# Semaphores cleared by ranges of numbers, and attention's gate steps laid by a written table

## The chip, the cores and the metric

One core of a Trainium2 chip runs the whole program. The metric is the device time of one execution in microseconds (us), as the median of several runs. The engines are named as the profile names them: PE multiplies matrices, PEld is its weight load, DVE is the vector engine, ACT the scalar engine, POOL the GpSimd engine, and SP only issues DMAs and handles semaphores.

## The reference, cut to what matters

The program is one layer of a sequence model: 2048 tokens of width 1024 are normalised, projected, mixed by three branches (pooling, differential attention, a state-space layer), gated, projected out, and sent through 32 experts. The change touches the attention stage and what stands between the stages.

```python
def block(args):                       # 16 blocks of 128 queries, 4 heads, 2 maps each
    qi, i = args
    s = jnp.einsum('bqhmd,bkhmd->bhmqk', qi, kf)
    p = jax.nn.softmax(jnp.where(mask, s, -1e30), axis=-1)
    a = p[:, :, 0] - lam * p[:, :, 1]
    return jnp.einsum('bhqk,bkhe->bqhe', a, vf)
o = lax.map(block, (qb, jnp.arange(nb)))
o = rmsnorm(o, subln_g) * (1.0 - lambda_init)
...
ga, gb, gc = jnp.split(jax.nn.sigmoid(h @ gate_w[l] + gate_b[l]), N_BRANCHES, axis=-1)
mixed = ga * (ya @ proj_a[l]) + gb * (yb @ proj_b[l]) + gc * (yc @ proj_c[l])
```

The mask is causal by blocks, so block i of queries meets keys 0 to 128 (i + 1) only. The product `h @ gate_w` doesn't depend on attention, and half of it is computed inside the attention stage.

## The kernel before, in words

**Stages.** Six stages follow one another: project, attention, pooling, ssm, out, moe. Each has its own semaphores and ends with `Stage.end` (L134): the engines have met at the end of the stage's block, SP clears each semaphore of the stage by an instruction of its own (L136), and all engines meet again (L137). Nothing of the next stage is issued before that. Semaphore numbers are handed out as they are asked for. The six stages hold 72, 36, 20, 47, 52 and 39 semaphores, whose numbers form 1, 1, 1, 2, 2 and 2 runs without a gap (project has 99 to 170; ssm has 153 to 170 and 227 to 255; moe has 171 to 204 and 222 to 226).

**Attention.** For each of 4 heads there are 16 items i (128 queries each). An item's keys are cut into pieces of up to 512, so item i has i // 4 + 1 pieces, and a head 40. In the step of item i, PE does this: the gate steps of the step's first slot; a wait until DVE has weighed item i (`weighed`, from L544); then, for each piece, the transposes of the item's scores (L321, into banks 4 and 5), perhaps up to two pieces of scores of item i + 2 (L311, banks 0 to 3), the gate steps of this piece's slot, and the product of the piece before with the values (L332, bank 6), which waits until ACT has copied the transposed piece (`place`, L437).

**The other engines in a step.** ACT goes in a fixed order: `take` of the last item (L442, L445); then, for each piece, `place`; behind it every `gate_out` that has come due (L420: it waits for the sum of 8 gate steps, and after every second one `w_high` rounds the next weights, L414); behind the first piece the exponentials of item i + 1 for map 1, and behind the second piece (or the only one) those for map 0 (L429). DVE reads scores out of the banks (L520, L523), takes maxima (L531, L532), turns the sums of the exponentials into factors (L539, L540) and weighs item i + 1 (L544); `lower` (L557) makes the low part of new gate weights.

**Gate steps.** One gate step is three matmuls of 512 columns (L344 to L346); 8 steps make a unit, which is summed in bank 7, and a head has 12 units. The first step of a unit waits until ACT has emptied bank 7 (`gate_placed`). `gate_plan` (L166) lays out how many steps stand in which slot: 8 ahead of item 0, 72 within the items, 8 behind item 15 and 8 behind the transposes of the outputs. A unit ends in these slots before (item, slot): (1,0) (2,0) (3,0) (4,2) (6,1) (7,2) (10,2) (13,1) (15,4). Slot 0 stands ahead of the wait for `weighed`, slot j ahead of the product of piece j - 1.

**Between heads.** PE does the 8 gate steps, then the scores of the next head's items 0 and 1, waits until DVE has read them out, waits for the normed outputs (`o_normed`, from L601), transposes them into banks 0 to 3 (L402), does 8 gate steps, and transposes the next head's values in four groups over banks 4 and 5 (`turn_v`, L358). Group 2 waits until ACT has copied group 0 out (L450). ACT does `take`, the square root (L488), `gate_out`, the exponentials, then the copies of the transposed outputs (L498).

**SP.** It stores gates and loads the next gate weights into one buffer (`load_w`, L256, in `store_gates`). At unit `units_by(NT - 3)` of a head it first waits until all scores of the head are made and then issues 16 loads of 256 KB for the next head's queries and keys (L252; in the last head two loads of 2 MB, L278 and L279). That unit is 9 before.

Of the kernel before, what the change touches and what calls it, by code (L numbers as in the profile page):

```python
# [25 lines left out]
KD = D // P  # L26
NT = T // P
TB = T // 512
EPS = 1e-6
HEADS = 4  # L30
# [74 lines left out]
class Stage:  # L105
# [26 lines left out]
        return s.__enter__()  # L132

    def end(self):  # L134
        for s in self.sems:
            self.nc.sync.sem_clear(s)  # L136
        self.nc.all_engine_barrier()  # L137


# [26 lines left out]
def gate_plan():  # L166


    wanted = [7] * 4 + [5] * 4 + [3] * 8
    first, last = KD, 2 * KD  # L170
    slots, placed, owed = [], first, 0
    total = 12 * KD
    for i in range(NT):
        n = i // 4 + 2
        row = []
        for j in range(n):
            owed += wanted[i] / n
            room = KD - placed % KD
            take = min(int(owed + 1e-6), room, total - last - placed)
            if i == NT - 1 and j == n - 1:  # L180
                take = min(total - last - placed, room)
            row.append(take)
            placed += take
            owed -= take
        slots.append(row)
    return first, slots


def stage_attention(nc, g, h_hi, h_lo, late_hi, late_lo, wt):

    RING = 3
    CH, NU = 6, 12
# [22 lines left out]
    with Stage(nc, "att") as s:  # L215
# [27 lines left out]
        with nc.Block() as block:  # L243
# [53 lines left out]
            @block.tensor  # L297
            def _(pe):
                def score(h, p):
                    i, c, width, _ = pairs[p]  # L300
                    gp = NP * h + p
                    if c == 0 and i % 4 == 0:
                        pe.wait_ge(qk_ready[i // 4], 64 * (h + 1))
                    if gp >= 2:
                        pe.wait_ge(q["evacuated"], 2 * gp - 2)
                    if h >= 1 and p in (2, 3):
                        pe.wait_ge(q["o_split"], 4 * h)
                    for a, b in ((q_hi, k_hi), (q_hi, k_lo), (q_lo, k_hi)):
                        for m in range(2):
                            own = slice(m * DH, (m + 1) * DH)  # L310
                            mm = pe.matmul(bank[p % 2 * 2 + m][:, :width], a[own, i * P:(i + 1) * P],  # L311
                                           b[own, c * 512:c * 512 + width], start=b is k_hi and a is q_hi, stop=a is q_lo)
                            if a is q_lo:
                                mm.then_inc(q["scored"], 1)

                def turn_a(h, n):
                    i, c, blocks = turn_units[n]
                    if n >= 2:
                        pe.wait_ge(q["a_placed"], NP * h + n - 1)
                    for j in range(blocks):  # L320
                        mm = pe.transpose(bank[4 + n % 2][:, j * P:(j + 1) * P],  # L321
                                          S[:, (NT * h + i) % RING, 0, (4 * c + j) * P:(4 * c + j + 1) * P], const(g, "ident"))
                    mm.then_inc(q["a_turned"], 1)

                def weigh_v(h, n):
                    i, c, blocks = turn_units[n]
                    if c == 0 and NT * h + i >= 1:
                        pe.wait_ge(q["o_copied"], NT * h + i)
                        pe.wait_ge(q["o_squared"], NT * h + i)
                    pe.wait_ge(q["a_placed"], NP * h + n + 1)  # L330
                    for j in range(blocks):
                        mm = pe.matmul(bank[6][:, 0:P], aT[:, n % 2, j, :], val[:, 4 * c + j, :],  # L332
                                       start=4 * c + j == 0, stop=4 * c + j == i)
                    mm.then_inc(q["summed"], 1)

                def gate(gn):
                    gu, k = gn // KD, gn % KD
                    c, tb = gu // 2, gu % 2
                    b, at = c % 2, slice(tb * 512, (tb + 1) * 512)
                    if k == 0 and tb == 0 and c >= 1:  # L340
                        pe.wait_ge(q["w_split"], c)
                    if k == 0 and gu >= 1:
                        pe.wait_ge(q["gate_placed"], gu)
                    pe.matmul(bank[7][:], w_hi[b][:, k, :], h_hi[:, k, at], start=k == 0, stop=False)  # L344
                    pe.matmul(bank[7][:], w_hi[b][:, k, :], h_lo[:, k, at], start=False, stop=False)  # L345
                    mm = pe.matmul(bank[7][:], w_lo[b][:, k, :], h_hi[:, k, at], start=False, stop=k == KD - 1)  # L346
                    if k == KD - 1:
                        mm.then_inc(q["gate_summed"], 1)

                def turn_v(h):  # L350
                    pe.wait_ge(q["v_ready"], 16 * (h + 1))
                    for t in range(TB):
                        if t >= 2:
                            pe.wait_ge(q["v_placed"], TB * h + t - 1)
                        elif h >= 1:
                            pe.wait_ge(q["a_placed"], NP * h - 1 + t)
                        for j in range(4):
                            mm = pe.transpose(bank[4 + t % 2][:, j * P:(j + 1) * P],  # L358
                                              vT[:, t * 512 + j * P:t * 512 + (j + 1) * P], const(g, "ident"))
                        mm.then_inc(q["v_turned"], 1)  # L360

                done = 0
                for h in range(HEADS):
                    if h >= 1:
                        turn_v(h)
                    while done < NU * KD * h + first_fill:
                        gate(done)
                        done += 1
                    if h == 0:
                        for p in range(first_pair[2]):  # L370
                            score(0, p)
                        turn_v(0)
                    pe.wait_ge(q["v_placed"], TB * (h + 1))
                    for i in range(NT):
                        ahead = list(range(first_pair[i + 2], first_pair[i + 3])) if i + 2 < NT else []
                        lo, hi = first_pair[i], first_pair[i + 1]
                        for _ in range(slots[i][0]):
                            gate(done)
                            done += 1
                        pe.wait_ge(q["weighed"], NT * h + i + 1)  # L380
                        for n in range(lo, hi + 1):
                            if n < hi:
                                turn_a(h, n)
                            for p in scored_in(n - lo, ahead):
                                score(h, p)
                            if n < hi:
                                for _ in range(slots[i][1 + n - lo]):
                                    gate(done)
                                    done += 1
                            if n > lo:  # L390
                                weigh_v(h, n - 1)
                    while done < (NU * h + 11) * KD:
                        gate(done)
                        done += 1
                    if h + 1 < HEADS:
                        for p in range(first_pair[2]):
                            score(h + 1, p)
                        pe.wait_ge(q["evacuated"], 2 * NP * (h + 1) + 2 * first_pair[2])
                    for c in range(4):
                        pe.wait_ge(q["o_normed"], 4 * h + c + 1)  # L400
                        for j in range(4):
                            mm = pe.transpose(bank[c][:, j * P:(j + 1) * P], o[:, 4 * c + j, :], const(g, "ident"))  # L402
                        mm.then_inc(q["o_turned"], 1)
                    while done < NU * KD * (h + 1):
                        gate(done)
                        done += 1

            @block.scalar
            def _(act):
# [46 lines left out]
                for h in range(HEADS):  # L456
# [29 lines left out]
                    take(NT * h + NT - 1)  # L486
                    act.wait_ge(q["o_squared"], NT * (h + 1))
                    nc.scalar.activation(ss[:], ss[:], ACT.Sqrt, scale=1.0 / P, bias=eps[:]).then_inc(q["o_rooted"], 1)  # L488
                    done += KD
                    while placed < done // KD:  # L490
                        gate_out(placed)
                        placed += 1
                    if h + 1 < HEADS:
                        exps(NT * (h + 1), 1)
                        exps(NT * (h + 1), 0)
                    for c in range(4):
                        act.wait_ge(q["o_turned"], 4 * h + c + 1)
                        nc.scalar.activation(S[:, (NT * h + NT - 1) % RING, 0, c * 512:(c + 1) * 512].bitcast(F32R), bank[c][:], ACT.Copy,  # L498
# [2543 lines left out]
```

## Time and profile before

| what | us |
|---|---|
| median of 3 runs | 3021.23 |
| the 3 runs | 3019.71, 3021.23, 3022.82 |
| the profiled execution | 3012.69 |
| its span, first to last instruction | 3010.8 |
| PE busy in the span | 2787.0 |
| attention, from 467 to 1135 | 668 |

The span leaves out 1.9 us of the profiled execution. The page gives each engine's busy time and a strip of 40 slices; the trace can be asked for waits, for a line's instructions, and for the instructions of a short window in order of time. A matmul's end is modelled: in an unbroken stream of 512 columns each is shown 0.39 us long though the next starts 0.227 us after it, so a true pause is some 0.16 us longer than the idle time that is listed.

### The profile page before, as it was taken

The numbers are of one execution on the slowest core, as the hardware profiler recorded it, in microseconds if no ns is written. First come the engines' busy times: TensorE is split into PE (matmuls) and PEld (weight loads), VectorE is DVE, ScalarE is ACT, GpSimd is POOL, SyncE is SP. The second block draws the span as 40 slices with busy tenths as digits, with TensorE's granted clock in tenths as the row PEclk, the third lists the DMA queues.
The fourth block names the chain that finished last, engine by engine and source line by source line (L and its number), as shares of the span: only waits on it lengthen the run. The fifth ranks groups of instructions, "written<-read, shape, count | busy, mean of one in ns | idle before, by whom it ended". The sixth has DMA issues, their size and how long they took to land. (4 is left out here: it accounts for less than half of the span.)

```text
span 3010.8 us, 41527 instructions
## 1 busy us (share of the span) xinstructions
PE 2787.0 (93%) x13642; PEld 2213.6 (74%) x13643; DVE 1904.8 (63%) x3149; ACT 1469.1 (49%) x2361; POOL 371.4 (12%) x287
## 2 busy tenths in 40 slices
PE   7999998989898997999997989995999999999996
PEld 5778886777777775888875877874777777777774
DVE  6655673636464554544555664347888888888874
ACT  5415653656555552233343332123666666666662
POOL 2101220000000001110110001110222222222211
PEclk9999998999999998999998999997999999999997
DMA  7465334141413127211148996526988998777884
GB/s 257 150 220 192 107 103 140 35 139 36 135 41 119 46 100 238 73 53 46 56 172 256 311 316 231 194 105 221 364 271 290 368 332 275 255 225 229 281 261 127
DMA packets 288834, 554.83 MB, mean 184 GB/s; under 512 B 28716, under 2 KB 95532, under 8 KB 285112
## 3 DMA queue, kind: packets, MB, share of 16 engines
q1 hardware_dynamic: 270296, 492.06, 47.3%
q0 software_dynamic: 14400, 52.44, 7.1%
q10 hardware_dynamic: 4000, 8.53, 0.9%
q8 instruction: 82, 1.34, 0.2%
q14 instruction: 56, 0.46, 0.1%
HBM read 418.21 MB, written 143.15 MB: 186 GB/s over the span
## 5 line engine op out<-in xcount | busy, mean ns | idle before, releaser
L2715 DVE TENSOR_TENSOR moe_w_lo<-moe_W,moe_w_hi 128x1024 fp32r<-128x1024 f32 x384 | 460.6, 1220 | 86.2 <-ACT moe_w_hi L2643 72.3
L2643 ACT CAST moe_w_hi<-moe_W 128x1024 fp32r (+1 forms) x384 | 402.0, 1053 | 152.7 <-PE moe_h1b L2566 77.1
L1630 PE MATMUL project_bank<-h_lo,w_hi 128*128 128x512 f32 x512 | 200.3, 391 | 0.0
L344 PE MATMUL att_bank<-h_hi,w_hi 128*128 128x512 f32 x384 | 170.7, 445 | 13.7 <-PEq L137 8.2
L2591 PE MATMUL moe_yb<-moe_W,moe_hT 128*128 x384 | 172.5, 592 | 0.0
L429 ACT ACTIVATE att_S<-att_S,att_nm,q_scale 128x128 f32<-128x128 f32 (+15 forms) x128 | 165.7, 1296 | 9.1 <-DVE att_nm L532 9.1
L2564 PE MATMUL moe_h1b<-moe_w_hi,moe_xT_hi 128*128 128x512 f32 x384 | 156.3, 407 | 4.8 <-DVE moe_xT_lo L2726 4.8
L523 DVE TENSOR_SCALAR_CACHE_REDUCE att_S<-att_bank 128x512 f32<-128x512 f32 x192 | 122.3, 686 | 53.2 <-PE att_bank L311 53.2
L346 PE MATMUL att_bank<-h_hi,w_lo 128*128 128x512 f32 x384 | 153.0, 398 | 0.0
L345 PE MATMUL att_bank<-h_lo,w_hi 128*128 128x512 f32 x384 | 152.9, 398 | 0.0
L332 PEld LDWEIGHTS att_bank<-att_val,att_aT 128*128 128x128 f32 x1088 | 137.4, 191 | 20.3 <-ACT att_aT L437 11.8
L2566 PE MATMUL moe_h1b<-moe_w_hi,moe_xT_lo 128*128 128x512 f32 x384 | 151.4, 394 | 0.0
L2565 PE MATMUL moe_h1b<-moe_w_lo,moe_xT_hi 128*128 128x512 f32 x384 | 151.4, 394 | 0.0
L332 PE MATMUL att_bank<-att_val,att_aT 128*128 128x128 f32 x1088 | 142.4, 276 | 8.3 <-ACT att_aT L437 8.3
L2566 PE MATMUL moe_h3b<-moe_w_hi,moe_xT_lo 128*128 128x512 f32 x384 | 149.6, 389 | 0.0
L2564 PE MATMUL moe_h3b<-moe_w_hi,moe_xT_hi 128*128 128x512 f32 x384 | 149.4, 389 | 0.0
L2565 PE MATMUL moe_h3b<-moe_w_lo,moe_xT_hi 128*128 128x512 f32 x384 | 149.4, 389 | 0.0
L2720 DVE TENSOR_TENSOR moe_w_lo<-moe_W,moe_w_hi 128x1024 fp32r<-128x1024 f32 x96 | 117.2, 1222 | 25.2 <-ACT moe_w_hi L2650 24.3
L700 ACT ACTIVATE gate_out<-ssm_gate_bank,gate_bias 128x512 f32<-128x512 f32 x42 | 28.9, 688 | 209.5 <-PE ssm_gate_bank L716 205.4
L2132 PE MATMUL out_bank<-out_y_hi,out_w_hi 128*128 128x512 f32 x256 | 102.9, 402 | 28.6 <-DVE out_w_lo L2021 12.3
L2591 PEld LDWEIGHTS moe_yb<-moe_W,moe_hT 128*128 128x128 f32 x384 | 72.6, 189 | 72.8 <-issue 69.0
L311 PE MATMUL att_bank<-shared 64*128 64x512 f32 (+2 forms) x960 | 121.6, 381 | 2.4 <-DVE att_S L523 2.3
(498 smaller groups left out, 6847.1 us busy)
## 6 DMA issues: line engine op xcount, KB each, us to landing
moe_W<-in_moe_w SPq DMA_DIRECT2D x96, 2048.0 KB, 13.5
w_raw<-in_gate_w SPq DMA_DIRECT2D x48, 512.0 KB, 3.8
out_sg<-gateT SPq DMA_DIRECT2D x32, 768.0 KB, 11.2
gateT<-att_gates SPq DMA_DIRECT2D x48, 256.0 KB, 2.3
gateT<-gate_out SPq DMA_DIRECT2D x48, 256.0 KB, 2.4
early<-in_ada_w SPq DMA_DIRECT2D x8, 1024.0 KB, 12.3
project_spare<-in_x SPq DMA_DIRECT2D x16, 512.0 KB, 6.3
zT<-project_oz SPq DMA_DIRECT2D x32, 256.0 KB, 3.6
```

Of the source, the lines that this page charges most:

```text
L332: mm = pe.matmul(bank[6][:, 0:P], aT[:, n % 2, j, :], val[:, 4 * c + j, :], start=4 * c + j == 0, stop=4 * c + j == i)
L344: pe.matmul(bank[7][:], w_hi[b][:, k, :], h_hi[:, k, at], start=k == 0, stop=False)
L345: pe.matmul(bank[7][:], w_hi[b][:, k, :], h_lo[:, k, at], start=False, stop=False)
L346: mm = pe.matmul(bank[7][:], w_lo[b][:, k, :], h_hi[:, k, at], start=False, stop=k == KD - 1)
L429: nc.scalar.activation(S[:, at, m, :n], S[:, at, m, :n], ACT.Exp, bias=nm[:, at, m:m + 1], scale=g["q_scale"][:, item // NT, item % NT, m: ...
L1630: pe.matmul(bank[n % 4][:], w_hi[b][:, k, :], low[:, k, at512(tb)], start=False, stop=False)
L2564: pe.matmul(to[:], xT_hi[:, k, :], w_hi[:, at, part], start=k == 0, stop=False)
L2565: pe.matmul(to[:], xT_hi[:, k, :], w_lo[:, at, part], start=False, stop=False)
L2566: mm = pe.matmul(to[:], xT_lo[:, k, :], w_hi[:, at, part], start=False, stop=k == KD - 1)
L2591: mm = pe.matmul(yb[nh][:], hT[:, k - KS, :], raw_2(at_raw, k, nh * 512, 512), start=False, stop=k == KF - 1)
L2643: nc.scalar.copy(w_hi[:, slot(p, first), :], raw(at, p)).then_inc(q["w13_high"], 1)
L2715: nc.vector.tensor_tensor(w_lo[:, own, :], raw(at, p), w_hi[:, own, :].bitcast(F32), ALU.subtract).then_inc(q["w1_low" if p < 4 else "w3_l ...
```

## The change

`Stage.end` sorts the numbers of the stage's semaphores and clears each run of neighbouring numbers by one instruction. `gate_plan` returns a table written out by hand, with the same 8 steps ahead of item 0 and 72 within the items. `turn_v` takes the groups that it is to turn: for heads 1 to 3, groups 0 and 1 are turned, 4 gate steps follow, groups 2 and 3 are turned, and the other 4 steps follow. The next head's first scores move ahead of the 8 gate steps behind item 15, while the wait for their reading stays behind those steps. On ACT the next head's first exponentials move ahead of the `gate_out` of that unit.

```diff
     def end(self):
-        for s in self.sems:
-            self.nc.sync.sem_clear(s)
+        numbers = sorted(s.num for s in self.sems)
+        first = numbers[0]
+        for a, b in zip(numbers, numbers[1:] + [None]):
+            if b != a + 1:
+                self.nc.sync.sem_clear(range(first, a + 1))
+                first = b
         self.nc.all_engine_barrier()
...
 def gate_plan():
-    wanted = [7] * 4 + [5] * 4 + [3] * 8
-    first, last = KD, 2 * KD
...
+    first = KD
+    slots = [[3, 3], [2, 4], [4, 2], [2, 4],
+             [2, 2, 1], [3, 1, 1], [2, 2, 1], [1, 2, 2],
+             [2, 0, 1, 0], [1, 1, 1, 0], [1, 1, 1, 0], [2, 0, 1, 0],
+             [1, 0, 1, 1, 0], [1, 0, 1, 1, 0], [1, 0, 1, 2, 1], [2, 1, 1, 1, 0]]
     return first, slots
...
-                def turn_v(h):
+                def turn_v(h, ts):
                     pe.wait_ge(q["v_ready"], 16 * (h + 1))
-                    for t in range(TB):
+                    for t in ts:
...
                     if h >= 1:
-                        turn_v(h)
+                        turn_v(h, range(0, 2))
+                    while done < NU * KD * h + first_fill // 2:
+                        gate(done)
+                        done += 1
+                    if h >= 1:
+                        turn_v(h, range(2, TB))
                     while done < NU * KD * h + first_fill:
...
+                    if h + 1 < HEADS:
+                        for p in range(first_pair[2]):
+                            score(h + 1, p)
                     while done < (NU * h + 11) * KD:
                         gate(done)
                         done += 1
                     if h + 1 < HEADS:
-                        for p in range(first_pair[2]):
-                            score(h + 1, p)
                         pe.wait_ge(q["evacuated"], 2 * NP * (h + 1) + 2 * first_pair[2])
...
+                    if h + 1 < HEADS:
+                        exps(NT * (h + 1), 1)
+                        exps(NT * (h + 1), 0)
                     done += KD
                     while placed < done // KD:
                         gate_out(placed)
                         placed += 1
-                    if h + 1 < HEADS:
-                        exps(NT * (h + 1), 1)
-                        exps(NT * (h + 1), 0)
```

The slots before and after, per item. The slots in which a unit ends become (1,0) (2,0) (3,1) (5,0) (7,0) (9,0) (11,2) (14,2) (15,3), and `units_by(NT - 3)` becomes 8.

```
item   before         after            item   before            after
0      3 4            3 3              8      0 1 1 1           2 0 1 0
1      1 6            2 4              9      0 1 1 1           1 1 1 0
2      2 5            4 2              10     0 1 1 1           1 1 1 0
3      3 4            2 4              11     0 1 1 1           2 0 1 0
4      1 2 1          2 2 1            12     0 1 0 1 1         1 0 1 1 0
5      2 2 2          3 1 1            13     0 1 0 1 1         1 0 1 1 0
6      1 1 3          2 2 1            14     0 1 0 1 1         1 0 1 2 1
7      1 2 2          1 2 2            15     0 1 0 1 1         2 1 1 1 0
```

## Rows read from the trace of the kernel before

**Rows 1.** The page: busy time of PE, and its granted clock in 40 slices.
```profile
PE 2787.0 (93%) x13642; PEld 2213.6 (74%) x13643; DVE 1904.8 (63%) x3149; ACT 1469.1 (49%) x2361; POOL 371.4 (12%) x287
PEclk9999998999999998999998999997999999999997
```

**Rows 2.** L136 at each stage's end: count, ns min/median/max, first and last start.
```profile
L136 SPq EVENT_SEMAPHORE_RANGE_CLEAR  x72: 25/30/39, 462.6 to 466.7; - x72
L136 SPq EVENT_SEMAPHORE_RANGE_CLEAR  x36: 25/30/49, 1134.9 to 1137.4; - x36
L136 SPq EVENT_SEMAPHORE_RANGE_CLEAR  x20: 25/28/30, 1194.9 to 1196.0; - x20
L136 SPq EVENT_SEMAPHORE_RANGE_CLEAR  x47: 25/25/30, 1595.2 to 1597.9; - x47
L136 SPq EVENT_SEMAPHORE_RANGE_CLEAR  x52: 25/30/35, 2047.0 to 2050.4; - x52
L136 SPq EVENT_SEMAPHORE_RANGE_CLEAR  x39: 25/25/39, 3008.3 to 3010.5; - x39
```

**Rows 3.** Instructions in order of time, PE, behind the first stage's end [idle before <- releaser].
```profile
467.02 0.77 PE L344 MATMUL att_bank<-h_hi,w_hi 128*128 128x512 f32 x1 [8.23 <-PEq L137]
472.71 0.62 PE L345 MATMUL att_bank<-h_lo,w_hi 128*128 128x512 f32 x1
473.40 0.39 PE L344 MATMUL att_bank<-h_hi,w_hi 128*128 128x512 f32 x1
```

**Rows 4.** In order of time: from head 0 to head 1, then the end of head 3.
```profile
626.81 0.96 PE L311 MATMUL att_bank<-shared 64*128 64x128 f32 x12
630.56 3.42 PE L402 MATMUL att_bank<-consts,att_o 128*128 128x128 f32 x16 [2.79 <-DVE att_o L601]
...
1121.36 1.91 PE L402 MATMUL att_bank<-consts,att_o 128*128 128x128 f32 x16
```

**Rows 5.** In order of time: the values' groups 2 and 3 of head 1.
```profile
641.65 1.15 PE L358 MATMUL att_bank<-consts,att_vT 128*128 128x128 f32 x8 [1.32 <-ACT att_val L450]
```

**Rows 6.** Waits in attention: us in total, times, longest us.
```profile
PE att_bank L321 <- DVE att_S L544: 17.5, 24, 1.5
PE att_bank L402 <- DVE att_o L601: 8.4, 3, 2.8
PE att_bank L332 <- ACT att_aT L437: 8.3, 8, 1.7
PE att_bank L344 <- ACT att_gates L420: 4.8, 7, 0.9
PE att_bank L358 <- ACT att_val L450: 4.2, 4, 1.3
```

**Rows 7.** In order of time: item 7's end and item 8's start, head 1.
```profile
711.56 0.66 PE L321 MATMUL att_bank<-consts,att_S 128*128 128x128 f32 x4 [1.48 <-DVE att_S L544]
```

**Rows 8.** In order of time: items 3 and 4 of head 1.
```profile
671.15 0.60 PE L321 MATMUL att_bank<-consts,att_S 128*128 128x128 f32 x4
675.60 0.39 PE L346 MATMUL att_bank<-h_hi,w_lo 128*128 128x512 f32 x1
```

**Rows 9.** In order of time: item 6 of head 1, a unit that ends in slot 1.
```profile
695.14 0.39 PE L346 MATMUL att_bank<-h_hi,w_lo 128*128 128x512 f32 x1
695.57 0.69 ACT L420 ACTIVATE att_gates<-att_bank,gate_bias 128x512 f32<-128x512 f32 x1 [1.89 <-PE att_bank L346]
697.09 1.24 ACT L429 ACTIVATE att_S<-att_S,att_nm,q_scale 128x1024 f32<-128x1024 f32 x1
```

**Rows 10.** In order of time: item 14 of head 1.
```profile
771.23 2.09 ACT L429 ACTIVATE att_S<-att_S,att_nm,q_scale 128x2048 f32<-128x2048 f32 x1 [1.53 <-DVE att_nm L532]
773.94 1.16 PE L332 MATMUL att_bank<-att_val,att_aT 128*128 128x128 f32 x8 [1.70 <-ACT att_aT L437]
```

**Rows 11.** SP's issues, and DMA issues with the median us to landing, head 1.
```profile
774.66 2.05 SPq L252 DMA_DIRECT2D shared<-qk_lo  x2
w_raw<-in_gate_w SPq DMA_DIRECT2D x2, 512.0 KB, 3.7
```

More of the change, by code:

```diff
@@ L166, in gate_plan @@
 def gate_plan():
-    wanted = [7] * 4 + [5] * 4 + [3] * 8
-    first, last = KD, 2 * KD
[L171 to L185, printed above, removed]
+    first = KD
+    slots = [[3, 3], [2, 4], [4, 2], [2, 4],
[3 rows of a table added]
     return first, slots
@@ L371, in _ @@
                             score(0, p)
-                        turn_v(0)
+                        turn_v(0, range(TB))
                     pe.wait_ge(q["v_placed"], TB * (h + 1))
```

## The prediction

> **What bounds the kernel now.** I read the page first. PE is busy for 2787.0 of 3010.8 us and its granted clock stays near full [rows 1], so time can only come from work taken off PE or from PE's pauses; this change removes no matmul. There are two kinds of pause to look at: the ends of the stages, and the waits inside attention. The source view of L136 shows that SP clears 266 semaphores one after another, each 25 to 30 ns long but about 60 ns after the one before [rows 2]. All engines stand still meanwhile: PE's first matmul of attention comes after 8.23 us of idle time that the barrier ended [rows 3]. In attention, the view of waits names who ends PE's pauses [rows 6], and the instructions in order of time show where in a head they lie. The four heads are alike to some 0.1 us, so I worked on head 1 and counted by heads.
>
> **Part 1, the clears.** From the first to the last clear it is 4.1, 2.5, 1.1, 2.7, 3.4 and 2.2 us, in sum 16.0 [rows 2]. Afterwards there are 9 instructions. The profile's name for what runs today is already a range clear, of one number, so I take the same 0.06 us for a wider one: 0.5 us stays and 15.5 go. Nothing hides them, and whatever comes behind a barrier starts earlier, its DMAs too. No row shows a wide range. From below, the cost can't be less than today's single one, which gives 15.5; from above I take the recorded 30 ns for every number in the range, 266 x 0.030 = 8.0 us, so that 8.0 go. I take 15.5, since the 25 to 30 ns are the instruction's own and the rest is issue, and since one instruction is what the sequencer sees.
>
> The Trainium skill (Runtime: NRT & Kernel Launch, The ~15µs preamble/postamble breakdown) gives about 1.5 us for resetting 51 semaphores per engine at a program's end, which by my division is an estimate of 29 ns for each. If a range were cleared at that price, 7.7 us would stay and 8.3 go. No row here shows it.
>
> **Part 2, from head to head.** Between heads PE makes the next scores at 626.81 and starts the output transposes at 630.56, with 2.79 us idle listed; the sixteen take 3.42 us of room, where head 3, with gate steps straight ahead of them and no next scores, needs 1.91 [rows 4]. The waits show this three times, 8.4 us [rows 6]; with 0.16 us of modelled end each it is 8.9. The transposes start late because DVE reads the scores first and norms behind that. Now 8 gate steps (24 x 0.227 = 5.5 us) stand between the scores and the transposes. DVE needs some 4.8 us from the scores' start until the second norm is made (626.81 to 631.6), so the wait is covered and head 3's row is what the others should look like: 8.9 for the pause and 3.42 - 1.91 = 1.5 for the first transposition block. That second part is a mixture of waits for single norms (0.45 us in each of three heads) and of the clock: the transposes of head 0 start 0.21 us apart (3.42 / 16) where head 3's start 0.12 apart (1.91 / 16). I count 8.9 + 1.4 of waits, and 2.2 for the low clock, which I see in two of three head changes: 12.5 us. Bounds: 8.9 if the clock still falls, 13 if all goes. ACT's moved exponentials (two of 0.5 us and a table load of 1.3) now run under the gate steps, ahead of a `gate_out` that has to wait for these steps anyway.
>
> **Part 3, the values.** Groups 2 and 3 wait 1.32 us listed, 1.5 really, for ACT, which is at a `gate_out` and a `w_high` [rows 5]; three heads, 4.2 us with that of head 0, which stays [rows 6]. Four gate steps (2.7 us) between the pairs cover it. But their first step starts a new unit and waits for the `gate_out` of the unit before, up to 0.2 us. I count 3 x 1.3 = 3.9 us. Bounds 3.0 and 4.5.
>
> **Part 4, the table.** No gate step is added or removed, so PE's work stays and only pauses change. What a head loses now, with the 0.16 us added: item 5 waits 1.0 for its weighing, 6 waits 0.8 for `gate_out`, 7 waits 0.4, 8 waits 1.65 [rows 7], 11 waits 1.6, 14 waits 0.7 and then 1.9 and 0.5 for copies by ACT [rows 10], 15 waits 0.7. That is 9.2 us a head, and agrees with the rows of L321 and L332 over four heads, (17.5 + 24 x 0.16) + (8.3 + 8 x 0.16) = 31, plus gate waits and scores [rows 6]. Now each item with the new slots:
> - Items 5, 6, 7, 8 come free. Their waits come from a `gate_out` that ACT takes between `place` and an exponential; the units now end in slot 0 of items 5, 7 and 9, and two or three gate steps ahead of items 5 and 8 cover the weighing.
> - Item 4 gets a new wait. The unit now ends in slot 1 of item 3, which has a single piece, so both exponentials of item 4 stand behind `gate_out` and `w_high`. The row to go by is item 6: last matmul of the unit 695.14, first exponential 697.09, so 1.95 us [rows 9]. In item 3 the unit's last matmul is 4.45 us after the item's start [rows 8], the exponentials then start at 6.4 and 7.3, and 2.4 us later (rest of the exponential, factors, weighing) item 4 is weighed: 9.7 us after the item's start. PE is ready at 7.1. So it waits 2.6 us.
> - The wait of item 11 moves to item 12, since the unit that ends in (10,2) now ends in (11,2): 1.7 us.
> - Item 14: ACT is at the 2.09 us exponential and the copy until about 5.2 us into the item [rows 10], and the `gate_out` of the unit that now ends in (14,2) stands behind both. PE comes to the first step of the next unit at 2.9. It waits 2.4 us; the steps behind it then hide the rest, where 3.8 us were lost before.
> - Item 15: `place` of the last piece now stands behind `gate_out` and `w_high`, and `w_high` needs weights whose load SP now issues behind the 16 loads of the next head (unit 8 in place of 9). Those are issued over 12.8 us, to 776.7 [rows 11]; a load of 512 KB lands 3.7 us after its issue when the queue is free. I come to some 22 us after the last scores where 21.3 are to be had: 0.9 us.
> - Small ones, 0.5 us.
>
> Sum 2.6 + 1.7 + 2.4 + 0.9 + 0.5 = 8.1 against 9.2, so 1.1 a head and 4.4 us in all. Bounds for the four heads: -4 (the waits at items 4 and 14 each 1 us longer than worked out) and +15 (item 4's wait isn't there).
>
> **The clock.** Behind a stage's end PE runs at the lower of its two levels (1.2 of 2.4 GHz) for a while: at 467.02 and 472.71 a matmul is 0.77 and 0.62 us long, at 473.40 it is 0.39 again, and the 14 between cost 0.2 us each, 2.8 in all [rows 3]. With half of the idle time gone it may not fall that long: 0 to 2.8 for each of two stage changes in front of dense matmuls, I take 1.5 in all. Against that, the new waits of 2.6 and 2.4 us are as long as those that lowered the clock between heads; I take 2.0 back.
>
> **The sum.** 15.5 + 12.5 + 3.9 + 4.4 + 1.5 - 2.0 = 35.8 us. The profiled execution of 3012.7 would become 2976.9. The median of the runs lies 8.5 us above the profiled execution; I take the same step from it: 3021.2 - 35.8 = 2985.4 us, 1.2% less.
>
> **The rivals.**
> - *The table gains more.* If ACT is not the one that holds item 4, or PE comes later than I think, 10 us more go: 2975. For it: I worked the items out, each alone. Against: ACT's fixed order is in the code and item 6's row has the same order.
> - *A range costs by its numbers.* 8.0 us go in place of 15.5: 2993.
> - *New waits and the clock.* Each new wait of over 2 us lowers the clock, 8 times 1.5 us, and the copies of items 14 and 15 come a little later: 2998. For it: the clock fell in two of three pauses of 2.9 us.
> - *Slower.* The place is `w_high` of item 15. SP's wait for the last scores now stands ahead of `load_w`, and behind it come 16 loads; ACT in its order stands at `w_high`, behind it the copy of the last piece, and PE waits for that. From 22.7 us after the last scores each us that the weights are late costs 4 us in the four heads. To come out over 3027 it has to undo 35.8 and 6 more, so 10.5 us a head more than worked out, 3030. Against: the 16 loads land within 20 us of the last scores and the queue is in order.
> - *The clears stay.* If the numbers weren't adjacent, 15.5 us would stay: 3001. The numbers are as told above, so this is small.
>
> **How the numbers follow.** Forecast 0.52, more from the table 0.15, price by numbers 0.12, new waits and the clock 0.15, slower 0.03, clears stay 0.03. The forecast's own spread, from the bounds of its terms, is 2978 to 2992. The range leaves out the ends: from 2972 to 3000. A measurement of this kernel can tell some 0.2%, 6 us. Faster by more than that is everything but the rival that is slower and a share of surprises: faster 0.96, same 0.02, slower 0.02.
>
> **What would show it.** In the profile after, L136 should have 9 instructions and PE's idle time ahead of attention should be near 4.2 us; L402 should have no wait for L601 in any head and be some 1.9 us long; L358 no wait for L450 in heads 1 to 3; L321 should wait some 2.6 us at item 4 of each head, and no more at items 5 and 8; the first gate step of unit 9 should wait 2.4 us in item 14. I would be wrong if L136 took over 0.1 us an instruction, if item 4 had no wait, or if ACT waited for `w_raw` by more than 1 us.

## The result, and the profile after

| | median, us | runs, us | profiled execution | its span |
|---|---|---|---|---|
| before | 3022.11 | 3019.71 to 3022.89 | 3012.69 | 3010.8 |
| after | 2992.96 | 2987.02 to 3001.44 | 3001.11 | 2999.2 |

After takes 0.9913 of before (95% interval 0.9895 to 0.9930, which is 21 to 32 us). By the two medians it is 29 us less, where 35.8 were forecast: 2993.0 for 2985.4. The two profiled executions lie only 11.6 us apart, since before's was 9.4 us under its own median and after's 8.2 us above its own. So stages are compared, not spans.

The page of after, PE's busy time and its granted clock in 40 slices, answers to [rows 1]:

```profile
PE 2801.2 (93%) x13642; PEld 2230.2 (74%) x13643; DVE 1905.6 (64%) x3149; ACT 1468.2 (49%) x2361; POOL 371.2 (12%) x287
PEclk8999998999999998999998999997999999999998
```

The count of matmuls is the same; the busy time is 14 us higher. The same matmuls last longer, so PE spent more of this execution at its lower clock. The table says where (us from a stage's first matmul to its last; in brackets the time at the lower clock there; "between" is all that lies between the stages and behind the last; what lies ahead of the first matmul, some 7 us, is left out):

| | project | attention | pooling | ssm | out | moe | between |
|---|---|---|---|---|---|---|---|
| before | 451.4 (17) | 661.3 (20) | 53.2 | 390.6 (38) | 440.3 (31) | 938.5 (44) | 68.4 |
| after | 456.4 (27) | 651.5 (34) | 52.9 | 395.5 (50) | 443.5 (37) | 940.1 (47) | 52.8 |

The change shows in two places, 15.6 us less between the stages and 9.8 less in attention. Four stages whose instructions it doesn't touch (project, ssm, out and moe) took 14.7 us more, each with more time at the lower clock; pooling took 0.3 less. The waits of PE in attention answer to [rows 6] (us in total, times, longest us):

```profile
PE att_bank L324 <- ACT att_aT L435: 10.8, 7, 3.4
PE att_bank L313 <- DVE att_S L542: 9.7, 4, 2.4
PE att_bank L336 <- ACT att_gates L418: 8.1, 7, 1.4
PE att_bank L303 <- DMA shared<-qk_lo: 1.8, 1, 1.8
```

The 24 waits for a weighing have become 4, but those 4 are 2.4 us long each. Waits for the normed outputs and for the values' copies (in heads 1 to 3) are gone, as worked out. The wait for ACT's copy (`place`) is larger than before: 10.8 for 8.3 us, with single ones of over 3 us, which the forecast didn't have.

The clears, from the source view of L139 (count, ns min/median/max, first and last start; stages project, attention, pooling, ssm), answer to [rows 2]:

```profile
L139 SPq EVENT_SEMAPHORE_RANGE_CLEAR  x1: 156/156/156, 467.3 to 467.3; - x1
...
L139 SPq EVENT_SEMAPHORE_RANGE_CLEAR  x1: 85/85/85, 1125.8 to 1125.8; - x1
...
L139 SPq EVENT_SEMAPHORE_RANGE_CLEAR  x1: 58/58/58, 1183.1 to 1183.1; - x1
...
L139 SPq EVENT_SEMAPHORE_RANGE_CLEAR  x2: 53/68/82, 1587.2 to 1587.3; - x2
```

In order of time, PE at attention's start and at the change from head 0 to head 1, answers to [rows 3] and [rows 4]:

```profile
467.73 0.47 PE L336 MATMUL att_bank<-h_hi,w_hi 128*128 128x512 f32 x1 [4.28 <-PEq L141]
468.04 0.43 PE L337 MATMUL att_bank<-h_lo,w_hi 128*128 128x512 f32 x1
...
471.25 0.59 PE L336 MATMUL att_bank<-h_hi,w_hi 128*128 128x512 f32 x1
471.68 0.39 PE L337 MATMUL att_bank<-h_lo,w_hi 128*128 128x512 f32 x1
...
476.82 0.95 PE L303 MATMUL att_bank<-shared 64*128 64x128 f32 x12 [1.77 <-DMA shared<-qk_lo]
...
623.31 1.16 PE L324 MATMUL att_bank<-att_val,att_aT 128*128 128x128 f32 x8 [3.06 <-ACT att_aT L435]
624.40 0.95 PE L303 MATMUL att_bank<-shared 64*128 64x128 f32 x12
...
630.90 1.91 PE L400 MATMUL att_bank<-consts,att_o 128*128 128x128 f32 x16
```

Idle time ahead of attention is 4.28 us in place of 8.23. Eight matmuls behind it are 0.2 us slower, where 14 were, but the first scores, 24 matmuls later, then wait 1.77 us for `qk_lo`. The output transposes take 1.91 us with no wait ahead of them. But straight in front of the head change stands a new pause of 3.06 us, at the last product of item 15.

### The profile page after: what moved, and what is told of

The parts are those of the page before. It is cut to its first block and busy times, and to the rows that moved or that the text cites. A ratio compares the mean times of both kernels' runs of the same rounds, so it can differ in the third digit from the quotient of the medians.

```text
span 2999.2 us, 41273 instructions
## 1 busy us (share of the span) xinstructions
PE 2801.2 (93%) x13642; PEld 2230.2 (74%) x13643; DVE 1905.6 (64%) x3149; ACT 1468.2 (49%) x2361; POOL 371.2 (12%) x287
## 5 line engine op out<-in xcount | busy, mean ns | idle before, releaser
L324 PEld LDWEIGHTS att_bank<-att_val,att_aT 128*128 128x128 f32 x1088 | 137.7, 191 | 23.7 <-ACT att_aT L435 14.7
L324 PE MATMUL att_bank<-att_val,att_aT 128*128 128x128 f32 x1088 | 145.2, 278 | 10.8 <-ACT att_aT L435 10.8
L435 ACT COPY att_aT<-att_bank 128x512 f32<-128x512 f32 (+3 forms) x160 | 82.6, 516 | 102.1 <-PE att_bank L313 101.5
```

## The experiments

Each kernel was run beside the kernel before on the same chip. Times are medians; stage lengths come from each profiled execution.

**1. The clears alone.** The kernel before with the new `Stage.end`, and with attention as it was.

```diff
-        for s in self.sems:
-            self.nc.sync.sem_clear(s)
+        numbers = sorted(s.num for s in self.sems)
...
+                self.nc.sync.sem_clear(range(first, a + 1))
```

> The kernel before with the clears by ranges alone. Theory: the trace of after shows 9 clears of 31 to 156 ns, 0.8 us in all where 16.0 stood, so 15.2 us go and nothing else changes: ratio 0.995, some 3007 us, attention as long as before (661 us from its first to its last matmul). Rival: the shorter standstill also keeps PE's clock up at the stage changes, and the clears are worth most of the 29 us of the change: 0.992 or less.

Measured: 3003.7 us beside 3022.7, 0.9946 (0.9928 to 0.9964), 19.0 us less. Attention took 659.6 us (661.3 before). Between its stages and behind the last lie 53.5 us, for 68.4 before and 52.8 after. PE's waits in attention:

```profile
PE att_bank L325 <- DVE att_S L548: 17.5, 24, 1.5
PE att_bank L406 <- DVE att_o L605: 8.4, 3, 2.8
PE att_bank L348 <- PEq L141: 4.3, 1, 4.3
```

Attention's waits are those of [rows 6] to the tenth, and the barrier's pause is 4.3 us. The clears are worth what lies between the stages, 14.9 us here, and that is half or more of all that the change gives. I had expected 15.2; the 4 us beyond it are not shown to be more than scatter, since the interval reaches from 11 to 22 us.

**2. The head change without the new table.** After, with the slots that the formula of before makes.

```diff
-    slots = [[3, 3], [2, 4], [4, 2], [2, 4],
...
+    wanted = [7] * 4 + [5] * 4 + [3] * 8
...
```

> The changed kernel with the slots of before; the clears, the scores ahead of the gate steps and the split values stay. Theory: the new table loses in attention (waits of 2.6 us at item 4 and 3.3 us at item 15, and a low clock behind them) more than it gives at items 5 to 11 and 14, so this kernel is faster than the changed one by about 16 us: 2977 us, attention 635 us from its first to its last matmul. Rival (the forecast): the table is worth 4 us and this kernel is slower than the changed one by as much: 2997 us.

Measured: 2990.37 us, 0.9900 (0.9880 to 0.9919); attention 646.1 us, of which 14 at the lower clock. PE's waits:

```profile
PE att_bank L325 <- DVE att_S L554: 17.5, 24, 1.5
PE att_bank L336 <- ACT att_aT L447: 8.3, 8, 1.7
PE att_bank L315 <- DMA shared<-qk_lo: 1.7, 1, 1.7
```

The waits for outputs and copies of values are gone and the table's are all there. From the first experiment to this one attention lost 13.5 us, for a forecast of 12.5 + 3.9 = 16.4. With the new table on top (after) it is 651.5: in that profile the table costs 5.4 us where I forecast 4.4 of gain. The second profile of after (experiment 5) has 647.7, so there it costs 1.6. The medians, 2990.4 and 2993.0, can't be told apart, so no gain by the table shows. The expected 635 us for attention and 16 us less than after were wrong; I had mis-worked them.

**3. The weights ahead of the sixteen loads.** After, with the point at which SP waits for the last scores one item later, so that the load of the next gate weights goes out first.

```diff
-                        if u == units_by(NT - 3):
+                        if u == units_by(NT - 2):
```

> The changed kernel, but SP waits for the head's last scores and loads the next head's queries and keys at unit 9 as before, so that the load of the gate weights isn't behind them. Theory: the wait of 3.3 us for the copy of the last piece in heads 0 to 2 is a wait for these weights; it falls to some 0.3 us and the low clock behind it goes too: 11 to 14 us less than the changed kernel. Rival: ACT's order alone makes that wait (the gate unit and the rounding stand ahead of the copy): it stays over 2 us, and the time with it.

Measured: 2979.1 us, 0.9862 (0.9842 to 0.9883); attention 636.7 us, 14.8 less than after's. First after, the end of head 1 in order of time (SP, ACT and PE):

```profile
759.61 0.80 SPq L244 DMA_DIRECT2D shared<-qk_hi  x2
...
773.09 0.74 SPq L248 DMA_DIRECT2D w_raw<-in_gate_w  x1
...
778.75 0.69 ACT L418 ACTIVATE att_gates<-att_bank,gate_bias 128x512 f32<-128x512 f32 x1
782.50 1.04 ACT L412 CAST w_hi<-w_raw 128x1024 fp32r<-128x1024 f32 x1 [3.06 <-DMA w_raw<-in_gate_w]
783.45 0.58 ACT L435 COPY att_aT<-att_bank 128x512 f32<-128x512 f32 x1
...
784.08 1.16 PE L324 MATMUL att_bank<-att_val,att_aT 128*128 128x128 f32 x8 [3.15 <-ACT att_aT L435]
...
786.90 0.63 PE L337 MATMUL att_bank<-h_lo,w_hi 128*128 128x512 f32 x1
```

Then the same place in this kernel:

```profile
740.36 0.38 SPq L248 DMA_DIRECT2D w_raw<-in_gate_w  x1
...
762.48 0.94 SPq L244 DMA_DIRECT2D shared<-qk_hi  x2
...
773.00 0.69 ACT L418 ACTIVATE att_gates<-att_bank,gate_bias 128x512 f32<-128x512 f32 x1
773.58 1.04 ACT L412 CAST w_hi<-w_raw 128x1024 fp32r<-128x1024 f32 x1
774.52 0.59 ACT L435 COPY att_aT<-att_bank 128x512 f32<-128x512 f32 x1
...
774.12 2.19 PE L324 MATMUL att_bank<-att_val,att_aT 128*128 128x128 f32 x16
```

In after the load goes out at 773.09, behind sixteen others, of which six have not landed by then, and `w_high` starts at 782.50, so 9.4 us from issue to use. ACT stands 3.06 us at it, the copy that PE wants stands behind it in ACT's order, and PE idles 3.15 us; then the gate matmuls last 0.63 in place of 0.39 us. Here the load went out 33 us before its use, `w_high` follows `gate_out` at once, and PE runs through. This confirms the cause. Three such pauses (none in the last head, where only two large loads are in front) are 3 x 3.4 = 10.2 us, and the low clock behind them brings the rest.

**4. Item 4 freed.** After, with two gate steps moved from item 3 to item 4, so that the unit ends in item 4 and no longer ahead of its exponentials.

```diff
-    slots = [[3, 3], [2, 4], [4, 2], [2, 4],
-             [2, 2, 1], [3, 1, 1], [2, 2, 1], [1, 2, 2],
+    slots = [[3, 3], [2, 4], [4, 2], [2, 2],
+             [2, 3, 2], [3, 1, 1], [2, 2, 1], [1, 2, 2],
```

> The changed kernel with two gate steps moved from behind item 3 into item 4 (item 3: 2 2, item 4: 2 3 2), so that the unit ends ahead of item 4 and not between item 3's copy and item 4's exponentials. Theory: the 2.6 us at item 4 go in all four heads and the low clock behind three of them too: 13 to 15 us less than the changed kernel. Rival: ACT is late as a whole and the wait comes back at item 5 or 6: under 5 us less.

Measured: 2980.32 us, 0.9872 (0.9851 to 0.9893); attention 637.4 us, 14.1 less than after's. The row of after that this was made against, head 1 in order of time:

```profile
670.81 0.69 ACT L418 ACTIVATE att_gates<-att_bank,gate_bias 128x512 f32<-128x512 f32 x1 [3.65 <-PE att_bank L338]
671.40 1.04 ACT L412 CAST w_hi<-w_raw 128x1024 fp32r<-128x1024 f32 x1
672.33 0.92 ACT L427 ACTIVATE att_S<-att_S,att_nm,q_scale 128x640 f32<-128x640 f32 x1
...
673.25 0.91 ACT L427 ACTIVATE att_S<-att_S,att_nm,q_scale 128x640 f32<-128x640 f32 x1
...
674.74 0.89 DVE L542 SCALAR_TENSOR_TENSOR att_S<-att_S,att_rec 128x640 f32<-128x640 f32 x1
...
675.68 0.66 PE L313 MATMUL att_bank<-consts,att_S 128*128 128x128 f32 x4 [2.43 <-DVE att_S L542]
...
676.27 2.46 PE L303 MATMUL att_bank<-shared 64*128 64x512 f32 x12
```

This is the chain that was worked out ahead: gate_out, the rounding, both exponentials, the weighing, then PE. Behind the pause the twelve scores take 2.46 us; when the kernel was profiled again the same twelve, behind the same pause, took 1.49 us (experiment 5). Here the granted clock has fallen to the lower of its levels. So the pause costs some 1.6 us more than itself, in three heads of four of this execution (in two of four when the kernel was profiled again, experiment 5). In the experiment the wait for L542 is gone, while ACT's wait for the weights has grown, from 9.4 us in 3 times to

```profile
ACT w_hi L412 <- DMA w_raw<-in_gate_w: 12.7, 4, 3.9
```

Most of that growth is a wait of 2.55 us at 491.44 in head 0, for the load that is issued behind the stage's first sixteen. At the ends of heads 0 to 2 the three waits come to 10.1 us, for 9.4 in after, so little of what was won at item 4 is waited away there.

**5. After once more,** unchanged, to see how far its own profile repeats.

> The changed kernel once more, unchanged. Theory: the trace of the first run had 14 us more than the kernel before in stages that the change doesn't touch, where PE's clock was granted at its lower level for longer; that varies from run to run. Attention is 651 us again within 3, the pauses between stages are 15.5 us shorter than before, the other stages are within 8 us in all of those of the kernel before, and the runs spread over 10 us: median 2993. Rival: something in the change makes the untouched stages slower each time: ssm over 395 and project over 456 us again.

Measured: 2999.13 us beside 3020.36, 0.9935 (0.9916 to 0.9954). Project took 451.9 and out 439.3 us, as in before; attention 647.7; ssm again 395.3. With moe at 940.5 the four untouched stages took 6.2 us more than before's here, not 14.7: 8.5 us belonged to that one execution, while some 5 us in ssm came again. Attention is 3.8 us shorter than in the first profile, a little outside my 3: head 1 is 5.0 us shorter and head 0 1.6 longer. In head 1 no slow matmuls followed item 4's pause, and its last copy was waited for 1.28 us and not 3.15, since the weights landed 6.7 us after their issue and not 9.4:

```profile
672.57 0.66 PE L313 MATMUL att_bank<-consts,att_S 128*128 128x128 f32 x4 [2.43 <-DVE att_S L542]
673.16 1.49 PE L303 MATMUL att_bank<-shared 64*128 64x512 f32 x12
...
776.00 1.04 ACT L412 CAST w_hi<-w_raw 128x1024 fp32r<-128x1024 f32 x1 [1.20 <-DMA w_raw<-in_gate_w]
777.58 1.16 PE L324 MATMUL att_bank<-att_val,att_aT 128*128 128x128 f32 x8 [1.28 <-ACT att_aT L435]
```

The six runs spread over 19 us, from 2989.1 to 3008.3, with a median 6 us above the one expected. The change's gain by the two measurements is 29 and 21 us.

**6. One step moved.** After with the old table, and item 3 with [2, 5] for [3, 4]: the step that ends the unit is now the first of slot 1 of item 3, and no longer the last of slot 0.

```diff
+    slots[3] = [2, 5]
```

> The slots of before with the other changes kept, and one gate step of item 3 moved from ahead of the item to behind it (2 5 for 3 4), so that the unit ends in slot (3,1). Theory: item 4 then waits 3.3 us in each head, where it waited for nothing, since the same chain runs from a unit that ends 0.7 us later: attention 13 us longer than with the slots of before, 659 us, and up to 5 more where the clock falls. Rival: a single step is hidden: attention 646 us as with the slots of before.

Measured: 2991.02 us, 0.9901 (0.9881 to 0.9921); attention 648.1. No wait for the weighing of item 4. ACT and PE in order of time, head 1:

```profile
664.16 0.69 ACT L431 ACTIVATE att_gates<-att_bank,gate_bias 128x512 f32<-128x512 f32 x1 [1.56 <-PE att_bank L351]
664.75 1.04 ACT L425 CAST w_hi<-w_raw 128x1024 fp32r<-128x1024 f32 x1
665.68 0.92 ACT L440 ACTIVATE att_S<-att_S,att_nm,q_scale 128x640 f32<-128x640 f32 x1
...
665.00 0.47 PE L349 MATMUL att_bank<-h_hi,w_hi 128*128 128x512 f32 x1 [0.87 <-ACT att_gates L431]
```

My expectation of 3.3 us was wrong, and the reason is plain in the rows: 31 steps stood before this slot, so the first of its five ended the unit, at 664.16, and the other four covered ACT's chain. Only the step behind waited, 0.87 us. What counts is how much PE work follows the unit's last step, not the slot in which it stands. In after the unit's last step is the last of four in the same slot, and nothing covers the chain.

**7. Both mends together** (the edits of experiments 3 and 4).

```diff
-                        if u == units_by(NT - 3):
+                        if u == units_by(NT - 2):
...
-    slots = [[3, 3], [2, 4], [4, 2], [2, 4],
+    slots = [[3, 3], [2, 4], [4, 2], [2, 2],
```

> The changed kernel with both mends: item 3 with 2 2 and item 4 with 2 3 2, and the loads of the next head at unit 9. Theory: the two waits are apart from each other and add up: attention 623 us, 28 less than the changed kernel, the median some 2964. Rival: they overlap, since PE that comes earlier to item 15 waits longer for other things: attention 630 or more.

Measured: 2963.03 us, 0.9809 (0.9794 to 0.9824); attention 620.6 us, 30.9 less than after's, where the single ones gave 14.8 and 14.1. They add up, as expected. These two pauses with their clock are what kept the table from gaining: without them it is 25.5 us better than the old one (646.1).

**8. Two more unit ends moved.** On top of that, units that end in slot 0 of items 12 and 14, and steps taken from where they cover nothing.

```diff
-             [2, 0, 1, 0], [1, 1, 1, 0], [1, 1, 1, 0], [2, 0, 1, 0],
-             [1, 0, 1, 1, 0], [1, 0, 1, 1, 0], [1, 0, 1, 2, 1], [2, 1, 1, 1, 0]]
+             [2, 0, 1, 0], [1, 1, 1, 0], [1, 1, 1, 0], [1, 0, 0, 0],
+             [2, 0, 1, 1, 1], [1, 0, 1, 1, 0], [2, 0, 1, 2, 1], [1, 1, 0, 1, 1]]
```

> Both mends, and the units that ended in (11,2) and (14,2) made to end ahead of their items, in (12,0) and (14,0): item 11 with 1 0 0 0, item 12 with 2 0 1 1 1, item 14 with 2 0 1 2 1, item 15 with 1 1 0 1 1. Theory: the 1.4 us at item 12 fall to 0.7 and the 1.6 us at item 14 to 1.1, so 1 us a head: attention 619 us. Rival: with fewer gate steps behind item 14 its weighing is waited for instead: 623 us or more.

Measured: 2951.94 us, 0.9778 (0.9762 to 0.9794), 68 us less than the median of before (3020.36) and the best of all; attention 608.7, 11.9 less than with both mends, for an expected 4. PE's waits in attention, now those of the heads' starts:

```profile
PE att_bank L336 <- PEq L141: 4.3, 1, 4.3
PE att_bank L336 <- ACT att_gates L418: 2.6, 3, 0.9
PE att_bank L303 <- DMA shared<-qk_lo: 1.7, 1, 1.7
```

The waits for `gate_placed` (8.2 us in 7 times with both mends) fell to 2.6 in 3: those of item 14 are gone and those between the heads stay. Items 11, 12 and 14 are 0.5, 0.9 and 1.3 us a head shorter at equal gate work, 2.7 in all, where 1 was expected.

**9 and 10. Ssm's start shifted.** After, with 16 and with 30 further clears of one semaphore at the end of pooling, so that ssm starts some 0.9 and 1.8 us later behind the barrier. The question was whether ssm's 5 us hang on where it starts.

```diff
+        if self.name == "pooling":
+            for _ in range(16):
+                self.nc.sync.sem_clear(self.sems[0])
```

> The changed kernel with 16 more clears of one semaphore at the end of the pooling stage, some 0.9 us during which every engine stands still, so that the ssm stage starts that much later. Both profiles of the changed kernel had 50 us at the lower clock in ssm and 395 us from its first to its last matmul, against 37 to 43 us and 389 to 392 in the kernel before and in six others. Theory: how long the clock stays low there hangs on when ssm starts; shifted, it is 389 to 391 us in this kernel or in the one with the longer shift. Rival: something of the changed kernel itself makes ssm long, and it is 395 us in both.

> As the one before, with 30 more clears, some 1.8 us. Theory: ssm is 389 to 391 us from its first to its last matmul in at least one of the two shifts, and the time falls by up to 5 us in spite of the added standstill. Rival: 395 us in both, and the time rises by the 1.8 us.

Measured: 2993.45 us, 0.9909 (0.9884 to 0.9934), and 2990.29 us, 0.9902 (0.9878 to 0.9927). Ssm took 396.7 and 396.8 us, with 51 and 52 us at the lower clock: unchanged. The gap ahead of ssm grew from 4.4 to 5.3 and 6.2 us, so the shift was there. A shift of this size doesn't bring the 390 us back. The other half of the rival, that the time rises by the added standstill, is too small to be seen in medians of 2990 and 2993 us.

## Why the prediction was right or wrong, point by point

**Clears, 15.5 us: right.** The nine recorded instructions take 0.7 us in sum, and 15.6 us went from between the stages. The rival by numbers (8.0) is out: 72 numbers took 156 ns, which is neither the flat 60 ns that I took nor 30 ns each. The condition "L136 over 0.1 us an instruction" came true for the widest and cost nothing.

The Trainium skill (Runtime: NRT & Kernel Launch, The ~15µs preamble/postamble breakdown) led to an estimate of 29 ns for resetting one semaphore. Here a range of 72 took 2.2 ns for each, so that estimate doesn't hold for a range inside a kernel; the measurement decides.

**Head change and values, 12.5 + 3.9 us: right in mechanism, a little large.** L400 waits for no norm and takes 1.91 us as worked out. Experiment 2 gives 13.5 us for both, within the bounds (11.9 to 17.5). In front of head 0, which the change leaves alone, PE lost 1.1 us more: from attention's first matmul to its first item it took 15.2 us, where the kernel of the first experiment took 14.2 (the reason stands with the clock, below). Without that the two terms gave 14.6.

**Table, 4.4 us of gain: wrong in sign.** By stage lengths it cost 5.4 us (experiment 2) or, by the second profile, 1.6. The table below gives how much longer an item is in after than in before, with each gate step taken off at 0.681 us (3 x 0.227), since the steps only change places. An item is counted from the end of the matmul ahead of it, so that the wait it begins with is its own. "Worked out" is the prediction's wait after less its wait before.

| item | worked out, a head | head 1 | four heads | four heads, after once more |
|---|---|---|---|---|
| 5, 6, 7, 8, 11 together | -5.4 | -4.9 | -19.6 | -19.7 |
| 4 | +2.6 | +4.2 | +15.1 | +13.5 |
| 12 | +1.7 | +0.9 | +3.7 | +3.7 |
| 14 | -0.7 | -1.7 | -6.7 | -6.7 |
| 15 and the unit behind it | +0.2 | +4.5 | +13.4 | +11.6 |
| all others | +0.5 | -0.1 | -0.5 | -0.6 |
| sum | -1.1 | +2.9 | +5.4 | +1.9 |

The freed items gained nearly what was worked out. Item 4's wait is 2.43 + 0.16 = 2.6 us in all four heads, right to the tenth; the rest of its 4.2 is the clock. Item 14 waits 1.39 + 0.16 = 1.6 for 2.4: ACT was on time (the step stands at 767.89, 5.2 us into the item, for the 5.3 worked out), but PE is ready only 3.7 us into it, where I had 2.9. Item 12 became 0.9 us longer, for 1.7. Two terms failed in the other direction, and they are larger.

*Item 15, the term of 0.9 us.* It was 3.2 to 3.6 us in three heads (in the second profile 3.3, 1.4 and 3.6). I had the issue time right (773.09, sixteen loads over 13.4 us) and then added the 3.7 us of [rows 11], the median of loads that find a quiet queue. When this one was issued, six of the sixteen loads, 1.5 MB, had not landed, and its data was used 9.4 us after the issue. The last copy starts 24.4 us after the last scores (759.1), not 22. My own rival "slower" named this very chain and said from when each us costs four; I priced it with the wrong row. It also put the point from which a late load costs too late: ACT was ready for the weights 20.3 us after the last scores, not 22.7. The condition "ACT waits for w_raw by more than 1 us" came true and experiment 3 shows the cause. In the last head, with two large loads in front, there is no wait, so it is three heads and not the four of the prediction.

*The clock, the term of -2.0 us.* This is the term that was sized too small. Behind item 4 it fell in three heads of four (1.6 us each), behind item 15 in heads 0 to 2 (0.1, 1.6 and 3.2). That is some 10 us in this execution. My rival "new waits and the clock" (2998) had the mechanism at 12 us; it and the forecast share the outcome, which came in between. The +1.5 at stage changes came to nothing. Ahead of attention the clock did rise sooner in after (8 low matmuls for 14), but the first scores then waited 1.77 us for `qk_lo`. In the kernel of the first experiment 14 were low, and PE had no such wait, because it came to the scores 8.6 us after its first matmul and not 7.3. So the time won at the first matmuls was lost at the load of the first queries. Behind that wait the clock then fell 10.8 us after attention's first matmul, where it had fallen at 13.0 us in the kernel of the first experiment, and the values' transposes ran slower: the two make up the 1.1 us.

**The sum.** In the profiled executions it is 15.6 between the stages, 9.8 in attention, and 14.7 back in untouched stages. By medians, which depend less on one execution, it is 29 and, in the second measurement, 21. For attention the terms were 12.5 + 3.9 + 4.4 - 2.0 = 18.8, so 9.0 are missing there. Of these, 1.2 are missing from the head change and the values (attention is 15.2 us shorter in experiment 2 than in before, for 16.4), and 7.8 from the table and its clock, which cost 5.4 where they were to give 2.4. The largest misses are item 15 and the clock behind it (13.4 for 0.8 in the four heads) and the clock behind item 4 (4.7, where 2.0 stood for all of it). Items 12 and 14 gave 7.0 more than worked out, and the small items 2.5, while the freed items gave 2.2 less. Ssm's 5 us come on top.

The time came out inside the range because the clears and the head change, some 32 of the 35.8 us, were right or nearly so. It also lies on the 2993 of the rival that prices a range by its numbers, but that is luck: the trace rules that rival out.

**What stays open.** Ssm took 395 to 397 us in all four profiles with after's attention (after, after again, both shifted), and 388.7 to 392.3 in the eight others. The whole difference is clock: some 49 to 52 us at the lower level against 36 to 43. It falls at the same four places inside ssm, only stays low there for longer, 6.8 to 13.7 us in place of 6.8 to 10.2. Experiment 3, with the same table and another order of loads, lies between: it is the longest of the eight (392.3 us, 43 low) and also has 13.7 us at one place. The instructions are the same. A start later by 0.9 and 1.8 us didn't change it, so its cause isn't settled.

## What to carry to other kernels

Price a load that a change puts behind others by the loads that have not landed when it is issued, not by the median of its kind; here one line in the issue order was worth as much as the whole head change. When you lay work by hand into another engine's gaps, look at each point where a unit ends: what the in-order engine must do there, what stands behind that in its queue, and how much work the waiting engine still has left (in experiment 6 four steps, 2.7 us, covered most of the chain that cost 2.6 us in after). A pause of 2.4 to 3.4 us on PE often cost half as much again in clock here, so one long wait was worse than several short ones of the same sum. And take a second profile before a difference of a few us is read from stage lengths: attention alone differed by 3.8 us between two profiles of one kernel.

## What the runs showed of the hardware

- A clear of a range of semaphores took 58, 85 and 156 ns for 20, 36 and 72 numbers, so some 25 ns and 1.8 ns for each number; single clears start 60 ns apart.
- The granted clock's mean differs from execution to execution of one kernel (0.959 to 0.966), and the time goes with it: after took 2987.0 us at 0.965 and 3001.4 at 0.960, before 3012.5 at 0.966 and 3031.3 at 0.959. That is 14 to 19 us in work that is the same, half of the effect measured here. Compare stages, and look at time at the lower clock first.
- A load of 512 KB landed 3.7 to 5.1 us after its issue on a quiet queue (the median of [rows 11] is 3.7). Behind sixteen loads of 256 KB it took 6.7 us when five of them had not landed at its issue, 9.2 to 9.6 us with six, and 10.3 to 10.6 us with seven (heads 0 to 2 of after and of its repeat).
- Between item 0 of the first head and attention's end, pauses of 1.3 to 1.7 us didn't lower PE's clock. Of those of 2.4 to 3.4 us, 5 of 7 did in after, 4 of 6 in its repeat and 2 of 3 in before; in after that cost 1.6 to 3.2 us each. At attention's start it did fall with shorter ones: in before at 480.0, behind a pause of 1.54 us, and in after at 478.5, in the second of two pauses, of 1.77 and 1.56 us.
